# The stretch between the triangular inverse and the first expert, put in another order, in a one-layer streaming encoder

## What is computed

```python
h = rms_norm(x, norm_mix_g)
proj = h @ w_in                     # q, k, v, z, two gates, and the conformer's columns
# delta rule in chunks; the lower triangular system is solved once per chunk
sol = triangular_solve(I + m, [v * beta, k * beta * exp(g)], lower=True, unit_diagonal=True)
u, w = sol[..., :dv], sol[..., dv:]
v_new = u - w @ s
o = (q * exp(g)) @ s + (q @ k.T * decay) @ v_new
s = s * exp(g_last) + (k * exp(g_last - g)).T @ v_new
o = rms_norm(o, w_onorm) * silu(z)
c = silu(layer_norm(causal_dwconv(glu) + b_dw))
x = x + concat([o, c]) @ w_out
h = rms_norm(x, norm_ffn_g)
top_val, top_idx = top_k(h @ w_router + b_router, 4)      # of 32 experts
gates = softmax(top_val)
for each expert e, on its rows of h:                       # 32 experts
    glu, lin = split(rows @ w_gate_up[e] + b_gate_up[e])
    act = min(glu, 7) * sigmoid(1.702 * min(glu, 7)) * (clip(lin, -7, 7) + 1)
    x[rows] += gate * (act @ w_down[e] + b_down[e])
y = rms_norm(x, norm_final_g)
```

## Time and profile before

| what | us |
|---|---|
| median of 3 runs | 1253.27 (1252.3 to 1256.91) |
| the profiled execution | 1257.68 |
| its span in the profile | 1255.8 |
| PE busy | 1161.8 (93%) |
| DVE busy | 462.7 (37%) |
| ACT busy | 242.7 (19%) |
| POOL busy | 70.7 (6%) |

### The profile page before, as it was taken

One profiled execution on the slowest core, in us unless ns is written; L12 is line 12 of the kernel. 1 busy time (PEld: TensorE's weight loads), 2 busy tenths in 40 slices (PEclk: granted clock), 3 DMA queues, 4 the chain that ended last, 5 costly groups with the idle time before them and its releaser, 6 DMA issues.

```text
span 1255.8 us, 16546 instructions
## 1 busy us (share of the span) xinstructions
PE 1161.8 (93%) x6576; PEld 536.8 (43%) x6576; DVE 462.7 (37%) x902; ACT 242.7 (19%) x428; POOL 70.7 (6%) x75
## 2 busy tenths in 40 slices
PE   7999998998999999999889899999999999996996
PEld 3566698546343442423233333334333333333342
DVE  5989645226442313132222222332331313222225
ACT  2144455233110101111010101111010111101012
POOL 1100143423000000000000000000000000000000
PEclk9999999897899999999999999999999999999998
DMA  9411210058899999999999999999999999999994
GB/s 376 198 68 68 90 26 2 13 196 318 354 429 427 428 429 427 429 429 427 429 429 428 428 428 426 388 419 428 428 430 427 428 430 428 427 430 425 428 428 168
DMA packets 35080, 433.74 MB, mean 345 GB/s; under 512 B 4736, under 2 KB 5120, under 8 KB 9216
## 3 DMA queue, kind: packets, MB, share of 16 engines
q1 hardware_dynamic: 32624, 428.64, 81.2%
q0 software_dynamic: 800, 3.08, 0.7%
q10 hardware_dynamic: 1616, 1.45, 0.4%
HBM read 428.51 MB, written 4.65 MB: 345 GB/s over the span
## 4 chain that ended last, share of the span: by engine, by line
PE 53%; DMA 41%; DVE 3%; issue 2%; ACT 1%; SPq 0%; DVEq 0%
DMA ring<-in_w_gate_up 40%; PE bank L1945 18%; PE bank L1572 10%; PE bank L1968 6%; PE bank L1808 3%; PE bank L1884 2%; PE bank L1689 1%; PE bank L2049 1%; PE bank L1708 1%; PE bank L1706 1%; PE bank L1924 1%; PE bank L2053 1%; PE bank L1955 1%; PE bank L2093 1%; DMA hT<-in_xT 1%
## 5 line engine op out<-in xcount | busy, mean ns | idle before, releaser
L1945 PE MATMUL bank<-ring,win 128*64 128x512 f32 x1984 | 442.9, 596 | 42.7 <-DMA ring<-in_w_gate_up 41.6
L1945 PEld LDWEIGHTS bank<-ring,win 128*64 128x64 f32 x1984 | 139.4, 137 | 328.8 <-issue 236.9
L1968 PE MATMUL bank<-ring,win 128*64 128x512 f32 x992 | 222.2, 601 | 0.3 <-issue 0.3
L1388 DVE TENSOR_SCALAR win<-bank 128x512 f32<-128x512 f32 x32 | 22.1, 692 | 396.9 <-PE bank L1945 380.9
L1968 PEld LDWEIGHTS bank<-ring,win 128*64 128x64 f32 x992 | 70.2, 138 | 134.0 <-issue 127.9
L861 ACT ACTIVATE win<-win 128x512 f32<-128x512 f32 x32 | 20.2, 632 | 439.7 <-DVE win L1388 439.7
L869 ACT ACTIVATE win<-bank 64x512 f32<-64x512 f32 x62 | 36.7, 593 | 279.6 <-PE bank L1968 266.4
L1321 DVE TENSOR_TENSOR win<-win,qkvc 128x1024 f32<-128x1024 f32 x16 | 19.6, 1226 | 141.4 <-ACT qkvc L887 141.4
L1382 DVE TENSOR_TENSOR xt<-xt,bank 128x512 f32<-128x512 f32 x108 | 68.1, 681 | 3.1 <-PE bank L1918 2.1
L1924 PE MATMUL bank<-qkvc,win 128*128 128x512 bf16 x288 | 67.7, 380 | 1.6 <-DVE qkvc L1474 1.4
L1006 DVE SCALAR_TENSOR_TENSOR cb<-ring,par,cb 128x384 f32<-128x384 f32 x120 | 66.5, 611 | 0.8
(11 more groups left out here) (329 smaller groups left out, 1050.6 us busy)
## 6 DMA issues: line engine op xcount, KB each, us to landing
ring<-in_w_gate_up SPq DMA_DIRECT2D x127, 2048.0 KB, 24.4
ring<-in_w_down SPq DMA_DIRECT2D x63, 2048.0 KB, 21.7
win<-in_w_in SPq DMA_DIRECT2D x3, 2048.0 KB, 8.9
ring<-in_w_in SPq DMA_DIRECT2D x2, 2048.0 KB, 13.2
win<-in_w_out SPq DMA_DIRECT2D x2, 2048.0 KB, 8.3
ring<-in_w_gate_up SPq DMA_DIRECT2D x2, 1024.0 KB, 10.5
out_ss<-ring POOLq DMA_DIRECT2D x1, 2048.0 KB, 9.2
ring<-in_w_down SPq DMA_DIRECT2D x2, 1024.0 KB, 19.1
```

Of the source, the lines that this page charges most:

```text
L1388: dve.tensor_scalar(g_s, bank[low], LIMIT, None, ALU.min).then_inc(g, 1)
L1945: mm = pe.matmul(bank[half][a * BLK:(a + 1) * BLK], xs[:, k], ring[:, c:c + 512], start=False, stop=(k == KD - 1), skip_group_check=True)
L1968: mm = pe.matmul(bank[7][a * BLK:(a + 1) * BLK], actT[:, q * P + j * BLK:][:, 0:BLK], ring[:, c:c + 512], start=(k == 0), stop=(k == KD - ...
```

## The change

- The last two levels of the inverse (5 and 6) work on 32x32 and 64x64 blocks alone, without masked copies; their subtractions are made block by block. The reciprocal of the conformer's norm stands between them on DVE.
- After the inverse PE's order is v_new(0), w_rows(2), w_rows(1), state(0), outputs(0), own_states, v_new(1), v_new(2), outputs(1), state(1), outputs(2), states_of(0), and only then the output projection, which is split into its conformer half and its head half. The second states_of and the turns of `o` stand between the halves.
- The running streams' states are decayed and grown by one DVE instruction a head that reads PSUM. The state input and output are laid out so that four streams are one contiguous block; the store is two of 1 MB.
- The router reads transposes of `x` itself; the norm's gain is multiplied into the router's weights and its factor into the logits. The turns of `x` are L1914, its products L1925, the logits L1936, the places L1947. It runs tile by tile between the parts of the projection, and so do choose, places, first_hits and first_rows.
- The first expert's parts are loaded whole, each behind its own wait.
- The loop over extra blocks stands before pair 12.

```diff
-FIRST_PIECES = ((0, 0, 2), (3, 1, 2), (4, 0, 4), (1, 0, 2), (2, 0, 2), (3, 0, 1), (5, 0, 4))
+FIRST_PARTS = (0, 1, 4, 5, 2, 3)
+BLOCK_LEVELS = 5
+STATE_OF = (0, 2, 4, 6, 1, 3, 5, 7)
...
-            sp.wait_ge(s_conf, CC)
-            sp.wait_ge(s_sout, 16)
-            sp.wait_ge(s_stq, 32)
-            sp.wait_ge(s_oTd, NT)
...
+            for r in FIRST_PARTS:
+                if r == 0:
+                    sp.wait_ge(s_v, NT)
+                if r == 1:
                     sp.wait_ge(s_s, NB + 2)
+                if r == 4:
+                    sp.wait_ge(s_ot, NT)
+                if r == 5:
                     sp.wait_ge(s_bsplit, 1)
+                    sp.wait_ge(s_sout, 16)
+                if r == 2:
+                    sp.wait_ge(s_ssout, 32)
+                load_piece(sp, 0, r, 0, GQ if r < GU else DQ)
...
+                    if l >= BLOCK_LEVELS:
+                        pe.wait_ge(s_a1d, n + 1)
+                        for h in range(H):
+                            for a, b in block_pairs(l):
+                                mm = pe.matmul(heads(bank[2 * n])[b, h, a], tile4(mt_, n)[a, h, b], tile4(d_, n)[a, h, a],
+                                               start=True, stop=True)
+                        mm.then_inc(s_x, 1)
+                        continue
...
+            def grown(out, gain, before, done):
+
+                for h in range(H):
+                    ins = dve.scalar_tensor_tensor(out[:, h], out[:, h], before[:, h], gain[:, h * P:(h + 1) * P], ALU.mult, ALU.add)
+                    if h < H - 1:
+                        order.inc(ins)
+                ins.then_inc(done, 1)
...
-            for b in range(NB):
-                pool.tensor_tensor(smp4[:, b], smp4[:, b],
-                                   tile4(eg_, 2)[:, :, TS * b + TS - 1:TS * b + TS].to_broadcast([P, H, P]),
-                                   ALU.mult).then_inc(s_dec, 1)
...
-            pool.dma_start(ss_out.rearrange("b h k v -> k (b h) v"),
-                           s_smp.rearrange("p (b v) -> p b v", v=P)).then_inc(s_ssout, 16)
+            states_out(0)
             pool.wait_ge(s_bpart, 2)
             pool.tensor_tensor(braw[2 * NE:3 * NE, :], braw[2 * NE:3 * NE, :], bparts[2 * NE:3 * NE], ALU.subtract)\
                 .then_inc(s_brest, 1)
+            states_out(1)
...
+            def router(n, halves_=(0, 1)):
+                for a in halves_:
...
+                    pe.wait_ge((s_xta, s_xtd)[a], n + 1)
+                    for j in range(4):
+                        mm = pe.matmul(bank[ROUTER_BANK][j * NE:(j + 1) * NE, n * P:(n + 1) * P], wr[:, 4 * a + j, :],
+                                       hT3[:, 4 * a + j, n * P:(n + 1) * P], start=(a == 0), stop=(a == 1), skip_group_check=True)
...
+                link(dve.scalar_tensor_tensor(lg[:, n], sums, rr[:, n:n + 1], col("b_router", 0, NE), ALU.mult, ALU.add))
...
+            project(1, 1, CONFORMER)
+            project_heads(1, 0)
+            turn_x(0)
+            project_heads(1, 1)
+            router(0)
+            pe.wait_ge(s_x2, 1)
+            project(2, 0, (4, 5))
             logits(0)
-            turn_h(2)
+            project(2, 0, (6, 7))
+            turn_x(1)
+            project_heads(2, 0)
+            router(1)
...
-            with pe.Fori(MID + 1, NU - 2) as u:
+            with pe.Fori(MID + 1, LATE) as u:
```

More of the change, by code:

```diff
@@ L1238, in _ @@
+            residual(0)
+            gated(2)
+            dve.wait_ge(s_gff, 16)
+            dve.wait_ge(s_stq, 32)
+            x_high(0)
+            norm_factor(0)
+            h_rows(0)
+            residual(1)
             choose(0)
-            h_turned(2)
+            x_high(1)
+            norm_factor(1)
+            h_rows(1)
+            residual(2, (0,))
             choose(1)
+            place(0)
+            place(1)
+            first_hits(0)
+            first_hits(1)
+            dve.wait_ge(s_x2q, NT)
@@ L1241, in _ @@
+            dve.tensor_scalar(eps_half, ssq_half, 1.0 / D, RMS_EPS, ALU.mult, ALU.add).then_inc(s_x2q, 1)
+            residual(2, (1,))
+            x_high(2)
+            norm_factor(2)
+            h_rows(2, 0)
+            h_rows(2, 1)
             choose(2)
[L1243 to L1246 removed]
+            place(2)
@@ L1812, in turn_h @@
[L1812 to L1828 removed]
+                                   start=(k == 4), stop=(k == 3), skip_group_check=True)
@@ new lines, in logits, with places @@
+            def logits(n):
+                if n == 0:
+                    pe.wait_ge(s_x2, 3)
+                else:
+                    pe.wait_ge(s_m, n)
+                pe.wait_ge(s_re, n + 1)
+                pe.matmul(bank[LOGIT_BANK[n]][:, NT * P + n * NE:NT * P + (n + 1) * NE], rT[:, n * P:(n + 1) * P],
+                          cst[:, X_SEL:X_SEL + NE], start=True, stop=True).then_inc(s_lg, 1)
+            def places(n):
+                if n == 0:
+                    pe.wait_ge(s_masks, 3)
+                    pe.wait_ge(s_x2, 4)
+                pe.wait_ge(s_m, min(n, NT - 1) + 1)
+                if n == 2:
+                    pe.wait_ge(s_hp0, 2)
+                for m in range(min(n + 1, NT)):
+                    mm = pe.matmul(bank[PLACES_BANK][:, n * NE:(n + 1) * NE], strict_b if m == n else ones_b, mall[:, m],
+                                   start=(m == 0), stop=(m == min(n, NT - 1)))
+                mm.then_inc(s_pp, 1)
@@ L1830, in _ @@
             v_new(0)
+            w_rows(2)
             w_rows(1)
-            w_rows(2)
+            pe.wait_ge(s_ve, 1)
+            state(0)
             outputs(0)
-            state(0)
             own_states()
-            turn_o(0)
             v_new(1)
+            v_new(2)
             outputs(1)
             state(1)
+            outputs(2)
+            states_of(0)
             pe.wait_ge(s_conf, CC)
@@ L1878, in rows @@
+            places(1)
+            project(2, 1, (2, 3)).then_inc(s_mix, 1)
+            router(2, (0,))
+            turn_x(2, (1,))
+            router(2, (1,))
+            logits(2)
+            first_rows(0)
+            places(2)
+            places(NT)
+            first_rows(1)
+            first_rows(2)
             def rows(ks, hits, width, extra=False):
@@ L2147, in _ @@
                             pe.wait_ge(x_dve, x_at(i, V_ADD, V_ADD))
+            with pe.Fori(LATE, NU - 2) as u:
+                pair(u, False, n_extra + (2 * u - 1), more=YC_WIDE)
             pair(NU - 2, False, n_extra + (NE - 3), ahead=BLK, more=YC_WIDE)
```

510 lines of the change are left out of this document (273 added, 237 removed).

## The result

| what | before | after |
|---|---|---|
| median in us | 1253.62 (1252.3 to 1256.91) | 1234.99 (1234.19 to 1238.07) |
| the profiled execution | 1257.68 | 1234.19 |
| its span | 1255.8 | 1232.4 |
| first product of the first expert (L1945, now L2082) | 306.88 | 281.69 |
| span minus that start | 948.9 | 950.7 |

The ratio is 0.9852, with an interval of 0.9827 to 0.9878: 18.6 us faster. The forecast was 1230.0 with a range of 1221 to 1241. Its size and its sign were right, and it was 5.0 us too low.

What follows compares the result with a forecast made beforehand. Weights bound the experts and PE all ahead of them. Steps of −2.1, −5.9, −0.4 and −18.8 gave −27.2 us; with one loss −23.3, so 1253.27 became 1230.0 us, range 1221 to 1241.

Steps and rivals of the forecast that it cites:

- The end moves with the first product: Whole kernel: the end follows the first expert's first gate and up product us for us, 948.9 us behind it.
- Inverse, −2.1: Inverse levels 5 and 6 on small blocks: first v_new starts at 205.8 instead of 207.88, 2.1 us sooner.
- v_new to the first projection, 15.8: PE from v_new(0) to the first output projection: 15.8 us instead of 21.7, a gain of 5.9.
- loss (a): Clock falls for 9 us behind PE's wait of about 2.0 us ahead of v_new(0), costing 4.1 us.
- Projections, 47.5: Output projection with router work between its parts: 47.5 us against 47.9 before, a gain of 0.4.
- The waits costed at nothing: During the projections: PE's waits cost 0, as DVE and ACT, with 8.8 us of state updates, work behind 3.43 us groups.
- Last projection's end to the first product, 10.6: Tile 2's router tail up to the first expert: 10.6 us instead of 29.4, a gain of 18.8.
- First loads, nothing: First expert's weights: the last part lands near 265, 14 us ahead of its first product, so they cost nothing.
- the cover was 24 us: First weight loads: an issue must come 24 us later than laid out before PE waits for weights.
- Loss (b), 3.9: POOL's bias subtraction starts ahead of DVE's normed(1) and locks the shared SBUF port, costing 3.9 us or nothing.
- one loss: Likeliest case: one of losses (a) and (b) occurs, −23.3 us, giving 1230; chance 0.41.
- the lay-out without losses: Sum of the steps up to the first expert: −27.2 us, its first product at 279.6, time 1226; chance 0.18.

Runs made afterwards that it cites:

- the third: The changed kernel, unchanged, profiled a third time: median 1235.56 us, ratio 0.9853 to the kernel before.
- before again: The kernel before, unchanged, run and profiled a second time: 1253.82 us, first product of the first expert at 304.45.
- after again: The changed kernel, unchanged, run and profiled a second time: median 1236.56 us, ratio 0.985 to the kernel before.
- filled_recip_last: Changed kernel with 10 unread matmuls in PE's level 6 waits, DVE's reciprocal behind level 6, POOL's bias subtraction behind both state stores: 1231.92 us, ratio 0.9815.
- filled: Changed kernel with 11 unread 128x128 matmuls on PE ahead of level 6's products and v_new(0): 1231.14 us, ratio 0.9826.

## Why the prediction was right, step by step

- **The end moves with the first product.** Right: span minus head was 948.9, and is 949.3 to 950.7. The rule is not exact to the microsecond. The head gained 22.7 to 22.9 us like with like, and behind it 0.4 to 3.2 us were given back, in part by the 7.94 us of L2055 at the end. Up to 1.8 us of this scatter in the first experts of both kernels: from the head to the second wait for weights (461.08 in before, 435.95 in after) it is 154.2 to 154.3 us in before, after and the third, 152.8 and 152.5 in the two others. The heads alone would have given 1253.6 − 22.7 = 1230.9, so most of the missing 5 us lie behind the head or in the scatter of medians; by the pairs of medians of the two later jobs the change is worth 20.2 and 19.1 us. What of it belongs to the new order (the loop's place, the end) stays open.
- **Inverse, −2.1.** Measured −1.8, from the inverse to the first v_new: 42.87 in before again and 41.10 in after, 44.45 in before and 42.64 in after again. The sum was nearly right, one term was not: the price of a small product. The 64 records (32 products) of L1788 and L1790 in the 32x32 level start between 196.98 and 197.54, about 0.02 us a product and not 0.057. The first and the last of them, from PE's timeline of after:

```profile
196.98 0.21 PE L1788 MATMUL bank<-ring 32*32 32x32 f32 x1
...
197.54 0.19 PE L1790 MATMUL bank<-ring 32*32 32x32 f32 x1
```

  It made little difference, because level 6 was bound as laid out by DVE's reciprocal (with it moved, in filled_recip_last, the first v_new came 1.0 us sooner):

```profile
200.73 2.55 DVE L1184 RECIPROCAL ust<-ust 128x384 f32<-128x384 f32 x1
```

- **v_new to the first projection, 15.8.** It took 17.8 and 18.8 in after and after again, and 16.4 in the three profiles without a clock fall there. The difference is loss (a); the remaining 0.6 was mis-sized in the sum (0.37 us of `issue` ahead of L1886 is a part of it). With the loss in it the gain is 2.9 us (21.7 in before to 18.8 in after again), and 1.5 us from before again to after (19.3 to 17.8): before's own half clock was shorter there than in the profile the prediction read.
- **Projections, 47.5.** Measured 48.4 (221.92 to 270.28), so that 0.5 us are lost here where 0.4 were to be gained. The waits costed at nothing cost nothing: DVE's state updates of four streams took 4.21 us (4.4 laid out), behind PE's groups.

```profile
222.08 4.21 DVE L1216 SCALAR_TENSOR_TENSOR ring<-ring,bank 128x128 f32<-128x128 f32 x16
```

- **Last projection's end to the first product, 10.6.** Measured 11.4 (270.28 to 281.69), with four waits of 0.49 to 0.78 us where 0.47, 0.72 and 0.73 were laid out. That is −18.0 against the 29.4 of the profile read and −19.5 against before again, where the low clock cost more. router_end shows what this step rests on.
- **First loads, nothing.** Right at their place: first issue at 216.83 (216.6 laid out), all landed by about 266, 0 GB/s in 266–276, no wait. Whether the cover was 24 us, no run measured.
- **Loss (a), 4.1.** It occurred, at 1.4 to 2.4 us. The term that was mis-sized is the excess of a 9 us spell. The spell itself was 7 us in after and 10 in after again, but PE stood for DVE anyway in 0.58 and 0.55 us of each 2 in 200–204, and so lost nothing ahead of v_new (42.66 us from the inverse to it in filled, 42.64 in after again); the cost is behind 204, where PE works without a break. **Loss (b), 3.9.** It did not occur; produced on purpose it cost 4.1.
- **The forecast's case** was "one loss", and one loss there was, −23.3 forecast, −22.7 measured at the first product and −22.3 from the inverse. That it came so near is in part luck: the lay-out without losses was 2.6 us too short (0.3 in the inverse, 0.6 behind v_new, 0.9 in the projections, 0.8 at the end), and loss (a) was priced 1.7 us too high against the pair with the longer spell. Counted against the profiled run of before the forecast was 1234.4, and the profiled run of after was 1234.19, which is luck too; counted against the median it was 5.0 too low, as what is said under the first point was not in the sum.

## What to carry to other kernels

When one stream of weights sets the rest of a program, find the one instruction to which it is tied and lay out only the way to it; here that gave a gain of 22.3 us to within 1 us, though with errors of up to 2.6 us that cancelled. Work with long waits for another engine (router, top-k, norms) belongs between the matmul groups of a projection: moving it back cost 10 us of 19, more than its waits, with PE at half clock around them. Making matmuls smaller gained nothing here, since PE then waited for DVE and lost its clock. A profiled execution far above its median should be profiled twice before its stretches are used as prices. And before two profiles are compared, look for clock falls ahead of the edit: here two of them, of 1.7 and some 2.5 us, made heads look equal that were not.

## What was not expected of the hardware

- An operation of DVE on four columns, both inputs in SBUF, stood 3.51 us instead of 0.16 beside POOL's 4.06 us instruction, and one on 256 columns 3.21 instead of 0.42. They end 0.01 and 0.27 us behind POOL's.
- A lead of 0.12 to 0.13 us of DVE over POOL was the same in nine profiles of several kernels.
- The same wait of 2.12 us on PE was followed by half clock in some executions (the product behind it 3.65 us) and not in others (2.05).
- 64 records (32 products) of 32x32 in float32 started within 0.56 us.
- Eleven matmuls that nobody reads kept the clock at its full level over 8 us and gave back 1.4 to 2.4 us between v_new(0) and the first projection.
